# Softmax weights moved into the added row maxima, value products in column pairs, and decay sums as one bfloat16 product

## The reference

```
def masked_softmax(s, mask):
    s = jnp.where(mask, s.astype(jnp.float32), NEG)
    m = jnp.max(s, axis=-1, keepdims=True)
    p = jnp.exp(s - m) * mask
    return p / jnp.maximum(jnp.sum(p, -1, keepdims=True), 1e-30)
...
    o_c = jnp.einsum('bqghc,bcgd->bqghd', p_c.astype(dt), cv)     # compressed blocks
    o_s = jnp.einsum('bqghks,bqgksd->bqghd', p_s.astype(dt), sk[..., 1, :])   # selected blocks
    o_w = jnp.einsum('bqghj,bjgd->bqghd', p_w.astype(dt), wk[:, :, 1])        # window
    return gb[..., 0:1] * o_c + gb[..., 1:2] * o_s + gb[..., 2:3] * o_w
```

```
logd = jnp.where(causal, b[..., :, None] + a[..., None, :] - m_t[..., :, None], -jnp.inf)
S = jnp.einsum('bhtd,bhsd->bhts', qb, kb) * jnp.exp(logd)
```

## Time and profile before

| | |
|---|---|
| median of three runs | 2990.9 us (2987.84 to 2996.4) |
| the profiled execution | 2981.6 us, its span 2979.8 us |
| granted TensorE clock, mean over the span | 0.895 of full speed |
| busy, share of the span | PE 86%, PEld 73%, DVE 61%, ACT 35%, POOL 12% |
| chain that ended last | PE 80%, DVE 13%, ACT 2%, DMA 1% |
| prompt attention, layer 0 | 565.27 to 720.94 us; layer 1: 1838.98 to 1994.2 |
| mLSTM stage, layer 0 | 236.7 to about 283 us |

### The profile page before, as it was taken

The page is one execution under the profiler, slowest core; times in us unless marked ns, Lnnn a source line. Parts: engine busy times, 40 slices in busy tenths (PEclk is TensorE's granted clock), DMA queues, the critical chain, the costliest instruction groups (busy, mean ns, idle before and its releaser), DMA issues.

```text
span 2979.8 us, 39782 instructions
## 1 busy us (share of the span) xinstructions
PE 2576.6 (86%) x15930; PEld 2176.2 (73%) x15930; DVE 1806.9 (61%) x2049; ACT 1052.7 (35%) x1126; POOL 361.1 (12%) x160
## 2 busy tenths in 40 slices
PE   6997797797859999969986886977599999999993
PEld 5995685544659999969965854446488888888883
DVE  6743755467433113148626654684398989898895
ACT  4441000122322112134411001223277777777773
POOL 2330000000213333313300000001200000000001
PEclk9995887797879999989968977987799999999997
DMA  4210401310112244222204003101399999999993
GB/s 150 75 51 15 157 1 40 124 36 15 43 63 79 97 140 126 79 83 82 66 15 136 22 30 126 45 15 43 113 421 410 378 384 384 377 391 375 389 369 126
DMA packets 115995, 452.28 MB, mean 152 GB/s; under 512 B 12835, under 2 KB 47523, under 8 KB 86371
## 3 DMA queue, kind: packets, MB, share of 16 engines
q1 hardware_dynamic: 110882, 431.92, 39.7%
q0 software_dynamic: 2624, 9.44, 1.0%
q10 hardware_dynamic: 2304, 8.39, 0.7%
HBM read 415.00 MB, written 42.95 MB: 154 GB/s over the span
## 4 chain that ended last, share of the span: by engine, by line
PE 80%; DVE 13%; issue 2%; ACT 2%; DMA 1%; POOL 1%; another core or an unknown queue 0%; DVEq 0%; SPq 0%; ACTq 0%; POOLq 0%; PEldq 0%
PE ps_buf L497 29%; PE ps_buf L2253 11%; PE ps_buf L2257 6%; PE ps_buf L2284 5%; PE ps_buf L1146 3%; PE ps_buf L2290 3%; PE ps_buf L1155 2%; PE ps_buf L1608 2%; PE ps_buf L1567 2%; PE ps_buf L1556 2%; PE ps_buf L1573 1%; DVE cols_buf L1284 1%; PE ps_buf L823 1%; PE ps_buf L1137 1%; DVE h_buf L561 1%
## 5 line engine op out<-in xcount | busy, mean ns | idle before, releaser
L497 PE MATMUL ps_buf<-xh_buf,whl_buf 128*128 128x288 f32 x3648 | 661.3, 302 | 76.3 <-POOLq L165 39.5
L2375 DVE TENSOR_TENSOR ring_lo<-ring,high_buf 128x2048 fp32r<-128x2048 f32 (+2 forms) x288 | 594.6, 2108 | 52.4 <-ACT high_buf L2331 50.2
L497 PEld LDWEIGHTS ps_buf<-xh_buf,whl_buf 128*128 128x128 f32 x3648 | 547.8, 191 | 90.1 <-issue 65.6
L2331 ACT CAST high_buf<-ring 128x2048 fp32r<-128x2048 f32 (+2 forms) x288 | 502.9, 1764 | 128.3 <-PE ps_buf L2257 70.0
L497 PE MATMUL ps_buf<-xl_buf,whl_buf 128*128 128x288 f32 x1824 | 397.3, 300 | 0.0
L485 POOL TENSOR_TENSOR whl_buf<-arena,whl_buf 128x1024 fp32r<-128x1024 f32 (+1 forms) x114 | 294.7, 2585 | 599.2 <-ACTq L165 598.3
L482 ACT CAST whl_buf<-arena 128x1024 fp32r<-128x1024 f32 (+1 forms) x114 | 124.7, 1094 | 492.7 <-PE ps_buf L497 474.2
L497 PEld LDWEIGHTS ps_buf<-xl_buf,whl_buf 128*128 128x128 f32 x1824 | 297.8, 192 | 0.0
L2253 PE MATMUL ps_buf<-high_buf,xbh_buf 128*128 128x512 f32 (+1 forms) x768 | 290.0, 378 | 5.4 <-ACT high_buf L2331 5.4
L2253 PE MATMUL ps_buf<-high_buf,xbl_buf 128*128 128x512 f32 (+1 forms) x768 | 288.4, 376 | 0.0
L2257 PE MATMUL ps_buf<-ring_lo,xbh_buf 128*128 128x512 f32 (+1 forms) x768 | 196.9, 378 | 0.0
(11 more groups left out here) (491 smaller groups left out, 3627.1 us busy)
## 6 DMA issues: line engine op xcount, KB each, us to landing
ring<-d_moe_up SPq DMA_DIRECT2D x128, 1024.0 KB, 7.5
ring<-d_moe_dn SPq DMA_DIRECT2D x80, 1024.0 KB, 7.5
ring<-d_moe_up SPq DMA_DIRECT2D x64, 768.0 KB, 6.7
arena<-d_w_in SPq DMA_DIRECT2D x54, 512.0 KB, 3.5
arena<-d_w SPq DMA_DIRECT2D x44, 512.0 KB, 3.6
arena<-d_w SPq DMA_DIRECT2D x16, 704.0 KB, 4.1
arena<-d_pages_c SPq DMA_DIRECT2D x64, 128.0 KB, 2.1
cols_buf<-d_w_out SPq DMA_DIRECT2D x16, 512.0 KB, 3.5
```

Source lines behind the costliest of these rows:

```text
L497: last = nc.tensor.matmul(ps_buf[0:rows, b + a_, 0:HALF], w, m[:, a_ * HALF:(a_ + 1) * HALF], start=start, stop=stop)
L2331: ac.copy(high_part(n), ring[:, 2048 * slot:2048 * slot + unit_cols(n % BLOCK_UNITS)])\
L2375: ve.tensor_tensor(low_part(n), ring[:, at:at + unit_cols(n % BLOCK_UNITS)], high_part(n).bitcast(F32), ALU.subtract).then_inc(S("moe_lo"), 1)
```

## The change

Attention. ScalarE now computes the softmax sums in the pair stage: after VectorE's maximum, two exponentials for each pair (`total`, one for each g) with the negated maximum as bias and the sum as a second output (`weight`). A pair's banks are free after that, and three pairs of banks are in turn (`pair_banks`). From `weight` VectorE forms gate divided by sum, ScalarE its logarithm, and VectorE adds that to the negated maxima before they are split, so that the exponentials in the score stage come out already weighed. The gates' spreading, its copy, the columns of ones and the reciprocals over 512 columns go. `vrow` holds 64 columns for each g, and `weigh` writes the two g into the two partition halves of one bank, `4 + h`, where both branches and the compressed branch add up; the compressed value products now stand after the last sum and leave the bank open. `mrow_h` holds the rows twice, at partitions 0 and 64, so that the two g of L1573 use 64 rows each. VectorE's work in the score stage is a copy for each of 4 banks. Head order is now h outer, w inner.

mLSTM. The row term is split into three bfloat16 parts in `u_h` (rows 0, 32, 64 on), and one bfloat16 product with `sel_h` takes the place of the float32 product. VectorE gets six instructions of 4 partitions in `rows_third_dve`, and a clearing of `u_h` before.

The core of the diff:

```diff
-        vaug = late_h.take(2, 4, 4 * HD)
-        coef = late_h.take(512)
+        vrow = late_h.take(2, 4, P)
...
+            v(ve.memset(u_h[:, :], 0.0))
...
+            v(ve.tensor_copy(u_h[0:4, :], RU))
+            v(ve.tensor_tensor(r(RD1), RU, u_h[0:4, :], ALU.subtract))
+            v(ve.tensor_copy(u_h[32:36, :], r(RD1)))
+            v(ve.tensor_copy(mid_h, r(RD1)))
+            v(ve.tensor_tensor(r(RD1), r(RD1), mid_h, ALU.subtract))
+            v(ve.tensor_copy(u_h[64:68, :], r(RD1)))
...
-                    pe.matmul(o, onehot(h, n), cols[0:4, CGATE, t0:t0 + n], start=True, stop=False)
+                    pe.matmul(o, sel_h[:, h:h + 1].to_broadcast([P, n]), u_h[:, t0:t0 + n], start=True, stop=False)
...
-        HEADS = [(w, h) for w in range(2) for h in range(4)]
+        HEADS = [(w, h) for h in range(4) for w in range(2)]
-        C_TURN, C_WEIGH = 8, 16
+        C_TURN = 10
...
-                t0, n, b = P * i, P * (i + 1), 2 * (s_ % 2)
-                if s_ >= 2:
-                    pe.wait_ge(S("at_max"), s_ - 1)
+                t0, n, b = P * i, P * (i + 1), pair_banks(s_)
+                if s_ >= 3:
+                    pe.wait_ge(S("at_total"), s_ - 2)
...
-                    pe.matmul(ps_buf[:, b + g, at:at + n], head_h[:, j:j + 1].to_broadcast([P, P]),
-                              mrow_h[:, P * c:SEQ], start=False, stop=False)
+                    pe.matmul(ps_buf[:, b + g, at:at + n], head_h[lo:lo + 64, j:j + 1].to_broadcast([64, P]),
+                              mrow_h[lo:lo + 64, P * c:SEQ], start=False, stop=False)
...
+            def weigh(u, m):
+                pe.wait_ge(S("at_exp"), 3 * u + m + 1)
+                for c in ((0,), (1, 3), (2,))[m]:
+                    n = SEQ - P * c
+                    for g in range(2):
+                        lo = 64 * g
+                        last = pe.matmul(ps_buf[lo:lo + 64, 4 + h, P * c:SEQ], vrow[:, w, c, lo:lo + 64],
+                                         PTs[:, u % 2, g, CHUNK_AT[c]:CHUNK_AT[c] + n], start=False, stop=w == 1 and c == 2)
...
+            pe.wait_ge(S("at_c_PT"), 1)
+            pe.wait_ge(S("at_total"), len(PAIRS))
+            for h in range(4):
+                for g in range(2):
+                    pe.matmul(ps_buf[64 * g:64 * g + 64, 4 + h, 0:SEQ], cvbd[:, g, 64 * h:64 * h + 64],
+                              PcT[:, g, :], start=True, stop=False)
...
+                ac.wait_ge(S("at_max"), s_ + 1)
+                for g in range(2):
+                    j = 8 * w + 2 * h + g
+                    a(ac.activation(unused[:, 0:n], ps_buf[:, b + g, 0:n], ACT.Exp, bias=negmax[:, i, j:j + 1],
+                                    accum_out=weight[:, i, j:j + 1]), *([S("at_total")] if g else []))
...
+            ac.wait_ge(S("at_weight"), 1)
+            a(ac.activation(weight, weight, ACT.Ln), S("at_ln"))
...
+            ve.wait_ge(S("at_total"), len(PAIRS))
+            v(ve.reciprocal(weight, weight))
...
+            v(ve.tensor_scalar(weight, weight, 1e-37, None, ALU.max), S("at_weight"))
+            ve.wait_ge(S("at_ln"), 1)
+            v(ve.tensor_tensor(negmax, negmax, weight, ALU.add))
...
-                ve.reciprocal(coef[0:64], ps_buf[64:128, b, :]).then_inc(S("at_recip"), 1)
-                ve.reciprocal(coef[64:128], ps_buf[0:64, b + 1, :]).then_inc(S("at_recip"), 1)
...
+            ve.wait_ge(S("at_rows"), 1)
+            v(ve.tensor_copy(mrow_h[64:112, :], ps_buf[64:112, 1, 0:SEQ]), S("at_mrows"))
+            for h in range(4):
+                ve.wait_ge(S("at_pv"), 2 * h + 2)
+                v(ve.tensor_copy(hmix[:, 4 + h, 0:SEQ], ps_buf[:, 4 + h, :]))
```

More of the change, by code:

```diff
@@ L229, in build @@
                          ("h", 5 * 2 * 256), ("arena", ARENA), ("page", NB * PAGES),
-                         ("half", 64 + 64 + 8 + 96 + 64 + 32)):
+                         ("half", 64 + 64 + 8 + 96 + 64 + 32 + 8)):
             place[name] = at_
@@ L356, in build @@
         G = rows_sp.take(T)
-        rows_sp.take(120)
+        rows_sp.take(-rows_sp.at % 8)
+        u_h = put_at("u_h", T, place["arena"] + rows_sp.at, BF16)
+        rows_sp.take(T // 2)
         seg12 = rows_sp.take(4, 12)
@@ L445, in build @@
         PTs = sp5.take(2, 2, 1280)
-        gsb = sp5.take(2, 512)
+        sp5.take(1024)
         sp5b = Space(arena, 4 * 2048, 9 * 1024 + 256 + 4096 + 4 * 9 * CMP)
@@ L454, in build @@
         PcT = phase1.take(2, SEQ)
-        scaled = lo_c.take(512)
+        phase1.take(512)
+        unused = phase1.take(SEQ)
+        lo_c.take(512)
         early = Space(cols_buf, lo_c.at - 512, lo_c.at)
@@ L460, in build @@
         ctot = early.take(2, 16)
+        weight = early.take(4, 16)
         mrow_h = put_at("mrow_h", SEQ, place["cols"] + lo_c.at, BF16)
@@ L1486, in cmp_act @@
             for w, dst in enumerate((svt, wvt)):
-                a(ac.copy(vaug[:, w].rearrange("p i (b d) -> p i b d", d=HD)[:, :, 0::3, :],
-                          bank(4 + 2 * w).rearrange("p (i g d) -> p i g d", i=4, g=2)))
+                a(ac.copy(vrow[:, w].rearrange("p i c -> p (i c)"), bank(4 + 2 * w)))
                 a(ac.copy(dst[0:64, :], ps_buf[0:64, 5 + 2 * w, 0:P]))
@@ L1541, in set_banks, with pair_banks @@
             return 2 * ((k + 1) % 2)
-        def out_banks(u):
-            return 4 + 2 * (u % 2)
+        def pair_banks(s_):
+            return (0, 2, 6)[s_ % 3]
         def at_pe():
@@ L1629, in at_pe @@
                     last.then_inc(S("at_c_T"), 1)
-                if s_ == C_WEIGH:
-                    pe.wait_ge(S("at_c_PT"), 1)
-                    for h in range(4):
-                        for g in range(2):
-                            last = pe.matmul(ps_buf[64 * g:64 * g + 64, 4 + h, 0:SEQ], cvbd[:, g, 64 * h:64 * h + 64],
-                                             PcT[:, g, :], start=True, stop=True)
-                    last.then_inc(S("at_c_pv"), 1)
+            pe.wait_ge(S("at_c_PT"), 1)
[4 more added lines that the diff above has]
+                              PcT[:, g, :], start=True, stop=False)
             pe.wait_ge(S("at_stat"), 1)
             for i in range(PT):
-                last = pe.matmul(ps_buf[0:48, 0, P * i:P * i + P], stat_h[:, 48 * i:48 * i + 48], ident_h[:, :],
-                                 start=True, stop=True)
+                for g in range(2):
+                    last = pe.matmul(ps_buf[64 * g:64 * g + 48, g, P * i:P * i + P], stat_h[:, 48 * i:48 * i + 48],
+                                     ident_h[:, :], start=True, stop=True)
             last.then_inc(S("at_rows"), 1)
-            pe.wait_ge(S("at_max"), len(PAIRS))
-            pe.wait_ge(S("at_c_out"), 1)
             for u in range(len(HEADS) + 1):
@@ L1647, in at_pe @@
                         score_set(u, m)
-                    if u and m < 2:
+                    if u:
                         weigh(u - 1, m)
@@ L1652, in at_act, with total @@
             ac = nc.scalar
+            def total(s_):
+                i, w, h = PAIRS[s_]
+                n, b = P * (i + 1), pair_banks(s_)
+                ac.wait_ge(S("at_max"), s_ + 1)
+                for g in range(2):
+                    j = 8 * w + 2 * h + g
+                    a(ac.activation(unused[:, 0:n], ps_buf[:, b + g, 0:n], ACT.Exp, bias=negmax[:, i, j:j + 1],
+                                    accum_out=weight[:, i, j:j + 1]), *([S("at_total")] if g else []))
             ac.wait_ge(S("at_c_max"), 1)
             a(ac.activation(Pc, Pc, ACT.Exp), S("at_c_exp"))
-            ac.wait_ge(S("at_c_T"), 1)
-            a(ac.copy(PcT, ps_buf[:, 4:6, 0:SEQ]), S("at_c_PT"))
-            ac.wait_ge(S("at_c_pv"), 1)
-            a(ac.copy(hmix[:, 4:8, 0:SEQ], ps_buf[:, 4:8, 0:SEQ]), S("at_c_out"))
+            for s_ in range(len(PAIRS)):
+                total(s_)
+                if s_ == C_TURN:
+                    ac.wait_ge(S("at_c_T"), 1)
+                    a(ac.copy(PcT, ps_buf[:, 4:6, 0:SEQ]), S("at_c_PT"))
+            ac.wait_ge(S("at_weight"), 1)
+            a(ac.activation(weight, weight, ACT.Ln), S("at_ln"))
             ac.wait_ge(S("at_clear"), 1)
@@ L1667, in at_act @@
                         ac.wait_ge(S("at_pv"), u - 1)
[L1668 to L1676 removed]
+                    at, n = 512 * m, 256 if m == 2 else 512
+                    a(ac.activation(PTs[:, u % 2, :, at:at + n], ps_buf[:, b:b + 2, 0:n], ACT.Exp), S("at_exp"))
         def at_dve(v):
@@ L1713, in at_dve @@
                 top(s_)
-            ve.wait_ge(S("at_max"), len(PAIRS))
+            ve.wait_ge(S("at_total"), len(PAIRS))
+            v(ve.reciprocal(weight, weight))
+            branch = gates[:, 0:4, :].rearrange("p i (g h k) -> p i h g k", g=2, h=4)
+            for w in range(2):
+                half_ = weight[:, :, 8 * w:8 * w + 8].rearrange("p i (h g) -> p i h g", g=2)
+                v(ve.tensor_tensor(half_, half_, branch[:, :, :, :, 1 + w], ALU.mult))
```

(3 more changed lines are left out.)

55 lines of the change are left out of this document (13 added, 42 removed).

## The result

The changed kernel takes 2906.88 us (median of 4 runs, 2900.37 to 2913.74) where the kernel before takes 2993.65 in the same comparison: ratio 0.9707, 95% interval 0.9671 to 0.9743, a gain of 2.9%. Run again on another occasion it gave 0.9738 (0.9716 to 0.976). The interval, 2892 to 2914 on the same footing, reaches into the range, and the second occasion's 0.9738 is 2913, inside it: the miss of the range is narrow, the miss of the forecast is not. The profiled execution is 2913.74 us, its span 2911.9, granted clock 0.892.

The account below looks back on a forecast made before the run. PE holds 80% of the chain of waits, VectorE 13%. Per layer 12.5 + 5.8 - 38.9 - 1.3 - 8.6 = -30.5 us, -61 in all, takes the median from 2990.9 to 2930; range 2906 to 2960.

Parts of the forecast that it names:

- the three of prompt attention: Prompt attention, per layer: +12.5 us to the last sum, +5.8 from there to the first set, -38.9 for scores and tail.
- mLSTM's term: mLSTM decay sums: a head falls from 0.94 to 0.40 us, -8.6 a layer, bounds -7 and -11.5.
- The fifth tile: mLSTM decay sums: counted at nothing, because VectorE's products there are late already.
- Rival D: Hand-over and mLSTM: clock stays up through the first, rises in the second; -10 us a layer, 2910; chance 0.11.
- Pair stage: Prompt attention up to the last sum: ScalarE's exponentials with sums set the pace, +12.5 us a layer.
- a sign of being wrong: Pair stage: the forecast is wrong if ScalarE's exponential with a sum is not 0.92 us at 512.
- rival C: Pair stage: three banks don't overlap, each pair passes the engines in a row; +67 us a layer, 3064; chance 0.04.
- rival A: Pair stage: ScalarE's pace leaves PE gaps and the clock falls; +8.4 us a layer, 2947; chance 0.14.
- Hand-over: From last sum to first set: PE idles, then eight compressed value products at a lower clock take 6.8 us; +5.8 a layer.
- Score stage: Prompt attention's scores and values with tail: a head takes 7.3 us on PE, stage 60.0 against 98.8, -38.9 a layer.
- Rival B: Score stage: column halves don't run side by side when weights change every product; +18 us a layer, 2967; chance 0.05.
- Sample attention: Its start: PE comes from work, 2 to 3 us at the higher clock save 1.3 a layer, bounds 0 and -4.

Follow-up runs that it names:

- 4-row run: The changed kernel with the decay sums' bfloat16 product over 4 partitions instead of 128; ratio 0.9764 to the kernel before.
- run without the chain: The changed kernel with ScalarE's 64 sums no longer waiting for its own last exponential; 2895.66 us, ratio 0.9671 to the kernel before.
- two filled kernels: The changed kernel with compressed value products moved forward and nine or five useless products added; nine: ratio 0.9709 to the kernel before; five: 2897.28 us, one execution.

## Why the prediction was too small

What sets the pace in each stage was forecast rightly; the sizes were not. Of the 9 us a layer by which the terms fell short, mLSTM's was 6.3 and 4.6 too small and the three of prompt attention together 7.4 and 7.2; sample attention, which got no shorter, took 4.6 and 2.4 back.

**The step that failed: mLSTM's term.** The forecast put a head's decay sum at 0.40 after the change, -8.6 a layer; it measured 0.21, and -14.9 and -13.2, outside the term's own bound of -11.5. The 0.40 took the mask's cost of 0.21 and the new product's at the same price. But that 0.21 held a change of shape, from 4 rows to 128, and with the new product on 128 rows too, neither has one. The 4-row run shows it: with the shapes left as they were, a head takes 0.43, and the stretch is 8.2 and 4.9 shorter than before, where 8.6 was forecast. I weighed the cost of a change of shape for the score stage, where it speaks against the change, and did not look for the place where it speaks for it. The second part is the clock: 0.56 to 0.62 in the tiles instead of 0.50, worth 1.4 to 1.8 us a layer. The fifth tile, counted at nothing, gave about 0.8 (0.38 a head instead of 0.58).

Rival D had this clock as its second part, with a chance of 0.11, and its 2910 lies near the measured time. That is luck: its first part, the clock staying up through the hand-over, did not happen.

**Pair stage**, the second size that was wrong, in kind right: +9.5 instead of +12.5. ScalarE sets the pace, and a sum of 512 took 0.855 instead of 0.92, which the prediction itself had named as a sign of being wrong. Its price came from a sum of 576 columns followed by a copy, and the earlier trace rows has no two sums in a row. The waits for the sums stayed covered by the third pair of banks (rival C did not happen; with two pairs the stage was 17.5 longer), and the clock was at 2.4 GHz from 582 to 611, with PE busy 21.96 of 29.00 (rival A did not happen either).

**Hand-over**: +4.6 instead of +5.8. The idle time, the fall of the clock and the eight products are as described; they took 5.7 instead of 6.8. That the clock makes this stretch what it is, the run without the chain shows most plainly: at 1.00 the same products took 3.45.

**Score stage**: -42.1 instead of -38.9. Rival B did not happen: values of two g took 1.01 for 512 with a change of shape, where B had 1.8. A head took 6.98 instead of 7.3, since I added five changes of shape and subtracted none. Scores and rows of maxima now share a shape, and a head's four sets of scores took 2.56 instead of 3.04, 0.12 less each. The parts that got new changes cost 0.8 more than their prices without them (maxima 0.94 for 0.55, values 2.62 for 2.28, masks 0.86 for 0.8), where 0.5 had been added.

**Sample attention**: the gain of its first products is there (from its start to L1797, which is L1805 in the changed file, 6.0 us before and 4.7 after), but not at its end: in layer 0 the whole stretch lasts 53 to 56 us instead of 52 in seven profiles with the new attention, and 55 in the one of the mLSTM part alone, so the attention is not needed to lengthen it. In the two filled kernels it is 49.0 and 50.8. What moves it is open.

**What stays open.** The two profiled executions differ by 68 us, the timed medians by 87. Both profiled executions of before, 2981.6 and 2978.9, are quicker than its median, and each has one RWKV stage of 244; those of the changed kernel have none (250.5 to 257.2 in four). By profiles the RWKV stage is thus some 5 us a layer longer after the change. The run with the attention part alone has one of 243.5, and so has the 4-row run one of 245.4; no run with the 128-row product has. Counted over all twelve profiles, four of the eight stages without that product last 243 to 246 us and none of the sixteen with it is under 250, which chance alone would seldom give. How that product could lengthen a stage that it has no part in, by shifting its start against the clock or otherwise, no run here shows. The timed runs carry no trace, so why their medians differ by more than the profiles do stays open as well.

## What to carry to other kernels

When a product changes its number of rows, count the changes of shape on both sides of it, those that go as well as those that come: at 0.11 each they were as large as the product itself. A wait for an engine's own last instruction costs where that engine sets the pace: taking it out from between the sums gave 7.5 us a layer in the stage and 2.3 behind it, where the whole change gave some 43. Before moving TensorE work out of a gap, ask what the gap's end then runs at: here, of 2.8 us won in the gap, 1.7 were lost again to slow scores.
